# A decoder layer on eight cores: the recurrence's end without sample steps, one key mask earlier, the spatial gate's means subtracted earlier

## The reference, cut to what matters

```python
x = x + 0.5 * swiglu(rmsnorm(x, g_ffn1), w_ffn1_in, w_ffn1_out)
h = rmsnorm(x, g_mix)
u_a, v_a, q_b, k_b, v_b, g_b, lr_b, gate_a, gate_b = jnp.split(h @ w_in, IN_SPLITS, axis=-1)
# mixer A
u_a = jax.nn.gelu(u_a)
v_n = layernorm(jax.nn.gelu(v_a), ln_v_g, ln_v_b)      # (y - mean) * rsqrt(var + eps) * g + b
mixed = jnp.einsum('gts,ncsgd->nctgd', ws, vb) + bias  # vb: v_n in chunks of 128 positions
y_a = u_a * mixed
# mixer B, per head: S_t = diag(a_t) S_{t-1} + k_t^T v_t,  o_t = q_t S_t  (blockwise, exact)
o, s_new = gla_recurrence(q, k, v, log_a, s0, block)
y_b = rmsnorm(o, g_gla_out) * jax.nn.silu(g_b)
mix = sigmoid(gate_a) * (y_a @ w_proj_a) + sigmoid(gate_b) * (y_b @ w_proj_b)
x = x + mix @ w_out
x = x + 0.5 * swiglu(rmsnorm(x, g_ffn2), w_ffn2_in, w_ffn2_out)
x = x + (p @ w_ple) * sigmoid(rmsnorm(x, g_ple) @ w_ple_gate)
y = rms_final(x)
```

## Time and profile before

| what | value |
|---|---|
| median of 3 timed runs | 1668.87 us (1667.63 to 1670.02) |
| the profiled execution | 1666.47 us |
| its span, first to last instruction, slowest core (core 0) | 1664.9 us |
| spans of the eight cores | 1655.2 to 1664.9 us |
| mean granted clock of TensorE, core 0 | 0.981 |
| busy: PE, DVE, ACT, POOL | 96%, 41%, 31%, 9% |

### The profile page before, as it was taken

One profiled execution on the slowest core, in us unless ns is written; L12 is line 12 of the kernel. 1 busy time (PEld: TensorE's weight loads), 2 busy tenths in 40 slices (PEclk: granted clock), 3 DMA queues, 4 the chain that ended last, 5 costly groups with the idle time before them and its releaser, 6 DMA issues.

```text
span 1664.9 us, 22936 instructions; the slowest of 8 cores (1655.2 to 1664.9 us)
## 1 busy us (share of the span) xinstructions
PE 1593.3 (96%) x9276; PEld 876.5 (53%) x9276; DVE 676.5 (41%) x1220; ACT 514.4 (31%) x996; POOL 153.5 (9%) x171
## 2 busy tenths in 40 slices
PE   5999999788999999999999999999999999999995
PEld 2555544344455545544666665555566666666652
DVE  3212247548445221366422225664624542222366
ACT  3112135543323112236111213575321331111144
POOL 3001000000000000000010000000000000000027
PEclk8999999889999999999999999999999999999998
DMA  9996361867746457368654424236325335325303
GB/s 161 137 158 111 41 105 32 165 162 165 153 69 97 74 78 107 62 122 127 141 82 65 70 40 68 46 46 120 52 41 87 51 51 95 58 45 84 64 1 114
DMA packets 144169, 147.74 MB, mean 89 GB/s; under 512 B 4064, under 2 KB 140016, under 8 KB 144064
## 3 DMA queue, kind: packets, MB, share of 16 engines
q0 software_dynamic: 115936, 112.01, 45.0%
q1 hardware_dynamic: 28128, 34.27, 6.8%
HBM read 240.07 MB, written 17.40 MB: 155 GB/s over the span
## 4 chain that ended last, share of the span: by engine, by line
PE 87%; DVE 4%; ACT 3%; issue 3%; DMA 2%; DVEq 0%; ACTq 0%; SPq 0%; POOLq 0%
PE ps L512 60%; PE ps L593 18%; PE ps L613 2%; PE ps L731 2%; DVE s_tsg L1677 1%; DMA s_ring<-w_ffn_in 1%; PE ps L474 1%; DMA s_ring<-w_in 1%; DVE s_xn L1315 1%; DMA s_zone<-xT 1%; PE ps L533 1%; ACT s_Sb L1164 1%; DVE s_zone L1680 1%; PE ps L760 1%; DVE s_Sf L1455 1%
## 5 line engine op out<-in xcount | busy, mean ns | idle before, releaser
L512 PE MATMUL ps<-s_xn,s_ring 128*128 128x384 bf16 (+2 forms) x5216 | 936.6, 338 | 5.4 <-ACT s_tsg L1072 1.9
L512 PEld LDWEIGHTS ps<-s_xn,s_ring 128*128 128x128 bf16 x5216 | 509.2, 98 | 405.7 <-issue 4.7
L1362 DVE TENSOR_TENSOR s_zone<-s_tsg,ps 128x384 bf16<-128x384 f32 (+2 forms) x220 | 127.8, 584 | 451.3 <-PE ps L512 431.4
L593 PE MATMUL ps<-s_zone,s_ring 128*128 128x384 bf16 (+2 forms) x1760 | 308.9, 338 | 0.0
L1050 ACT ACTIVATE s_tsg<-ps 128x384 f32<-128x384 f32 (+2 forms) x220 | 112.4, 514 | 475.3 <-PE ps L512 460.5
L593 PEld LDWEIGHTS ps<-s_zone,s_ring 128*128 128x128 bf16 x1760 | 172.2, 98 | 134.7
L1004 ACT ACTIVATE s_sqr<-s_zone 128x384 bf16<-128x384 f32 (+2 forms) x163 | 86.8, 547 | 293.2 <-DVE s_zone L1377 223.1
L512 PE MATMUL ps<-s_zone,s_ring 128*128 128x384 bf16 (+2 forms) x800 | 158.9, 339 | 0.0
L1377 DVE SCALAR_TENSOR_TENSOR s_zone<-ps,s_zone 128x384 f32<-128x384 f32 (+2 forms) x80 | 47.0, 588 | 206.4 <-PE ps L593 206.4
L1072 ACT ACTIVATE s_tsg<-ps 128x384 f32<-128x384 f32 (+2 forms) x160 | 79.7, 510 | 164.6 <-PE ps L512 163.7
L512 PEld LDWEIGHTS ps<-s_zone,s_ring 128*128 128x128 bf16 x800 | 78.5, 98 | 61.9 <-issue 1.0
(11 more groups left out here) (151 smaller groups left out, 965.8 us busy)
## 6 DMA issues: line engine op xcount, KB each, us to landing
s_ring<-w_ffn_in POOLq DMA_DIRECT2D x38, 1024.0 KB, 13.4
s_ring<-w_in POOLq DMA_DIRECT2D x24, 1024.0 KB, 13.4
s_ring<-w_ffn_out POOLq DMA_DIRECT2D x16, 1024.0 KB, 11.0
s_zone<-st SPq DMA_DIRECT2D x13, 512.0 KB, 6.4
ss_out<-s_zone SPq DMA_DIRECT2D x13, 512.0 KB, 5.9
s_ring<-w_ffn_in POOLq DMA_DIRECT2D x12, 512.0 KB, 9.2
s_ring<-w_ffn_out POOLq DMA_DIRECT2D x8, 768.0 KB, 10.5
s_zone<-xT SPq DMA_DIRECT2D x6, 768.0 KB, 10.0
```

The lines of the kernel that those rows point to most:

```text
L512: ins = pe.matmul(ps[:, 0:n], piece[:, k, off:off + 128], rhs[:, k, :], start=(k == 0), stop=(k == nkc - 1))
L593: ins = pe.matmul(ps[:, 0:n], view[:, jj, c % 4 * 128:c % 4 * 128 + 128], h_v(t, j)[:, c0:c0 + n], start=(j == 0), stop=(j == JH - 1))
L1362: ins = dve.tensor_tensor(h_v(t, j)[:, c0:c0 + n], sg_of("f", f, t, j, si)[:, 0:n], bank("u", f, t, j, si)[:, 0:n], ALU.mult)
```

## The change

Four edits.

1. `STEPS_LOOP` is (2, 3, 4) instead of (3, 4, 5, 6) and `STEPS_VA` is (2, 5) instead of (3,): steps 0, 1 and 2 stand behind blocks 2, 3 and 4, none behind blocks 5 and 6, step 3 behind the v_A block of tokens 1, step 4 behind that of tokens 4. From step 5 on all stand where they stood. ScalarE's and VectorE's extra step behind the recurrence goes.
2. TensorE's `epi_sum` for the last block moves into the recurrence, behind the block's state increment (in the second group behind the v_A block there), ahead of one more v_A block than before. This holds for both groups.
3. Mask 1 is made beside mask 0, before the loop, and step 0 makes none. Later steps make the mask of the next step as before.
4. `centre` of all blocks comes ahead of the g products, on VectorE, in both groups; in the first one sample steps 5, 6 and 7 stand between them. Among the g products only `rescale` is left.

```diff
-STEPS_VA = (3,)
-STEPS_LOOP = (3, 4, 5, 6)
+STEPS_VA = (2, 5)
+STEPS_LOOP = (2, 3, 4)
...
                         epi_sum(t, b)
                         bank.drop("ro", t, b, 0)
                         bank.drop("ro", t, b, 1)
+                    else:
+                        epi_sum(t, b)
+                        bank.drop("ro", t, b, 0)
+                        bank.drop("ro", t, b, 1)
...
                     if i == len(VA_EARLY[t]):
                         for j in range(i):
                             bank.drop("va", t, ln_blocks(t)[j])
-                        epi_sum(t, NBLK[t] - 1)
-                        bank.drop("ro", t, NBLK[t] - 1, 0)
-                        bank.drop("ro", t, NBLK[t] - 1, 1)
...
                 epi_rms(t, NBLK[t] - 1)
-                if t == 0:
-                    sample_step()
...
-                if n + 1 < NS:
+                if 1 <= n < NS - 1:
                     make_kmask(n + 1)
...
                 if t == 0:
                     make_kmask(0)
+                    make_kmask(1)
...
                 epi_norm(t, NBLK[t] - 1)
-                if t == 0:
-                    sample_step()
...
                 if t == 0:
-                    for i in STEPS_U:
-                        sample_step()
                     dve.wait_ge(*const["lng"].at())
...
-                left = [(part, i, b) for i, b in enumerate(blocks) for part in (centre, rescale)]
+                for i, b in enumerate(blocks):
+                    centre(i, b)
+                    if t == 0 and i % 3 == 1:
+                        sample_step()
+                left = [(rescale, i, b) for i, b in enumerate(blocks)]
```

## The result

The changed kernel takes **1654.18 us** (median of three runs, 1651.15 to 1654.88) where the kernel before takes 1668.87 us (1667.63 to 1670.02). The ratio is **0.9912, 95% interval 0.9897 to 0.9926**: faster by 14.7 us (12.3 to 17.2). Forecast: 1653.3 us, 15.6 us less, with 0.90 for "faster". Some executions run 3 to 18% slower, at a lower granted clock on four or on all eight cores, and are left out of every time and ratio here. Sign and range held, and so did the total; the term for the centring in u did not, and the gain up to u was mis-sized by 0.9 us.

What follows compares the result with a forecast made beforehand. TensorE, busy for 96% of the span, was taken as the bound, its longest wait 7.9 us on ScalarE's gelu. Terms of 11.0 - 0.3 + 4.2 + 0.7 = 15.6 us off 1668.87 gave 1653.3 us, range 1648.5 to 1661.5.

Steps and rivals of the forecast that it cites:

- the term for the centring in u: First group's u products: eight mean subtractions ahead of sample steps 5 to 7 delay a bank, costing 0.3 us.
- the gain up to u: First group, end of the recurrence through the v_A blocks: the products for u begin 11.0 us earlier.
- (a): First group's recurrence: sample steps 0 to 2 one block earlier make block 4 wait for banks, costing 0.85 us.
- (b): Block 6: both idles before it stay, it starts at once at 319.2, its norm's sum waits 1.0 us.
- (c): v_A block 0 at the lower clock takes 3.5 us, to 327.5; ScalarE's first two gelus end at 328.9.
- (d): From block 6's sum TensorE runs without a gap, the clock rises at 328.5, u begins 11.0 us earlier.
- Rival 1: Around block 6 the clock does not fall, as less idle follows: 2.7 us more gained, 1650.6; chance 0.12.
- Masks: First group's sample steps: making mask 1 beside mask 0 moves an instruction and saves none, 0 us.
- Rival 2(a): VectorE and ScalarE later than charged, u's bank 1 us short twice included: some 7 us less gain, 1660; chance 0.20.
- Centring out of the g products: First group's silu(g) products: VectorE loses the mean subtractions there, TensorE's waits shrink, 4.2 us gained.
- Second group: Its v_A blocks: the norm's sum goes one block earlier, gelus start sooner, a 0.74 us wait goes; 0.7 us gained.
- Rivals 3 and 4: Clock falls at block 4: rising as forecast, about 1666, chance 0.05; or low through the v_A blocks, 1673, chance 0.03.

Runs made afterwards that it cites:

- sum_only: The kernel before with only the norm's sums of both groups' last blocks moved right behind the block: 1661.42 us, ratio 0.9965.
- the second timing: The changed kernel itself, timed once more beside the kernel before in five rounds: 1650.65 us, ratio 0.9901.

## Why the prediction was right, and where its steps were off

- **What bounds the kernel.** Right. The longest wait was the chain behind the late sum; moved, it is gone, and sum_only shows 4.9 us for it alone.
- **(a), steps one block earlier: charged 0.85 us, measured 1.45** (12.75 to 14.2 from block 2's sum to block 4's, within 0.1 us on every core). Inside the bounds of 0 to 2. "Fit into an idle moment of TensorE" was the weak step: the idle times in the stretch did not shrink but grew, from 2.1 to 2.5 us on core 0, and the extra step's 0.8 us of matmuls came on top. (They are missing behind block 4 in turn, so the two stretches up to u are to be read together.) The path was right up to the second half of v block 5, which waits for the bank that held the turned keys and starts 7.3 us behind block 2's sum (7.0 forecast). But block 4 then waits for ScalarE's copy of that half (L1120), not for VectorE's norm, which had ended 0.16 us before the copy:

```profile
301.94 1.90 PE L613 MATMUL ps<-s_ring,s_xn 128*128 128x512 bf16 x8 [0.69 <-ACT s_zone L1129]
...
304.79 0.22 PE L689 MATMUL ps<-s_PT,s_zone 128*128 128x128 bf16 x1 [0.40 <-ACT s_zone L1120]
```

- **(b), block 6.** The two idles stay, as said, 1.68 and 1.71 us; the second was forecast at 1.39. The forecast left out the 0.33 us that TensorE idled at block 6's first product behind the sample step; with the step gone the two stand together, 1.39 + 0.33 = 1.72. L716's new wait was put at 1.0 us and is 1.05.
- **(c) and (d), to u.** 11.0 us forecast from core 0. There it is 11.5 (57.2 to 45.8 us from block 2's sum to u), on the median of all cores 10.1 (55.9 to 45.8): core 0, the slowest before, was one of three (0, 2 and 6) on which the clock had been down without a break from ahead of block 6 to the long wait, and had 1.3 us more to lose. The clock was low for 6.8 us or less, not 9.5, and on five cores (3 to 7) part of what that won went into waits at the first two v_A blocks (0.33 and 0.95 us on core 4), which the forecast did not have. The forecast had the engines' order right and too little of their waits.
- **Rival 1, the clock does not fall.** It came true on two cores of eight (4 and 5). On the other six the clock fell as forecast, but for 6.8 us on three (0, 1 and 2) and half of that on three, not for 7 to 10; for the stretch that made no difference. The rival's price was mis-sized: 1.3 us (30.3 against 31.4 to 31.7 from block 4 to u), where 2.7 were worked out. And on these two cores it was given back in u, where the clock fell instead (51.6 us from u to gate A).
- **Masks: 0.** Right, and tested.
- **Centring in u: charged 0.3 us, measured 1.1 to 1.9 us of wait**, and on three cores (0, 4 and 5) the lower clock behind it. Cores 5 and 6 both wait 1.65 us; on core 5 the clock then falls, and the next sample step stands 16.2 us behind u's start, on core 6 14.5: 1.7 us for the fall. This is the step that failed. The text saw that each step could come "up to 2.0 us later" and named the right bank, but took VectorE's idle time as the cover; the idle time it read (4.12 us) stands before step 7, and step 5 has none, since the last statistics of v_A end just before the centring. Rival 2(a) had this at 1 us twice. By the forecast's own sign ("wrong if a product of u waits behind a sample's copy") it was wrong here; its total held because the gains elsewhere were far larger.
- **Centring out of the g products: 4.2 us forecast; 4.67 us of waits became 0.42, 4.25.** Right.
- **Second group: 0.7 us forecast, 0.9 measured.** The kernel's 82.2 against 81.3 us is the cleanest number of the study: all kernels with the early sum agree to 0.1 us.
- **Rivals 3 and 4, the clock falls at block 4.** It did not: for 20 us from block 2's sum on it was at 1.00 on all eight cores, in spite of six waits of 0.2 to 0.7 us. The rule that speaks for it (the Trainium skill, TensorE: Matmul & The Clock Gate, A second HAM failure mode: psum-queue depth-cycling) was not borne out there. In u a single wait for a bank of 1.2 to 1.9 us stands ahead of the lower clock on three cores of eight, and waits of 1.1 to 1.9 us do on the others without it; that is one wait and not the cycling that the page describes.
- **Sum.** 11.0 - 0.3 + 4.2 + 0.7 = 15.6 against, by the stretches, 12.6 from block 2 to gate A (10.1 up to u and 2.4 behind it, by medians) + 0.9 = 13.5. That the whole time came out at 14.7 and, in the second timing, at 16.5 us is nearer to the forecast than the steps deserve, and in part luck: the whole time moves by some us with the clock in places that the change does not touch.

## To carry to other kernels

When work is moved under a "cover" of idle time, read the idle time in front of the very instruction that is delayed, not an average or the largest one nearby, and put what others wait for (here a sample step) ahead of what nobody waits for. Work out a chain on more than one core when the clock differs between them; a stretch between two marks, taken on all cores, shows half a microsecond where whole runs show three. Short matmuls gathered in one place can cost clock although TensorE never idles; with free work on either side, deal them out among long ones, but only where the other engines have room.
